# Weights split four blocks deep, and a stage that ends and begins with four blocks by token halves

## The reference, cut to what matters

```
h    = rmsnorm(hres, g0);  m = mixer(h)            # layer 0: attention, layer 1: gated short convolution
hres = hres + rmsnorm(m, g1)                       # a "post norm"
h    = rmsnorm(hres, g2);  m = (relu(h @ w_up))**2 @ w_down
hres = hres + rmsnorm(m, g3)
```

## Time and profile before

| | |
|---|---|
| time, median of 3 runs | 1764.56 us (1763.05 to 1765.94) |
| the profiled execution | 1752.25 us, its span 1750.5 us |
| TensorE matmul busy | 1647.5 us, 94% of the span, mean granted clock 0.978 of full |
| VectorE, ScalarE, GpSimd busy | 771.9, 621.7, 623.2 us |
| raw weights moved | 225 loads of 512 KB |
| share of the chain that ended last | TensorE 79%, VectorE 12%, GpSimd 3%, waiting for nothing shown 3% |

### The profile page before, as it was taken

One profiled execution on the slowest core, in us unless ns is written; L12 is line 12 of the kernel. 1 busy time (PEld: TensorE's weight loads), 2 busy tenths in 40 slices (PEclk: granted clock), 3 DMA queues, 4 the chain that ended last, 5 costly groups with the idle time before them and its releaser, 6 DMA issues.

```text
span 1750.5 us, 31301 instructions
## 1 busy us (share of the span) xinstructions
PE 1647.5 (94%) x12544; PEld 1444.2 (83%) x12544; DVE 771.9 (44%) x1260; ACT 621.7 (36%) x1127; POOL 623.2 (36%) x315
## 2 busy tenths in 40 slices
PE   7999998889999999989998999999998999999895
PEld 6788886879999999989987788888887777777764
DVE  3333333274323141374435642323217897445536
ACT  5455655253223131242223432323224454222222
POOL 2222220354443443454434444444444434700011
PEclk9999997999999999999999999999999999999998
DMA  5111110212323223212222233222331222100001
GB/s 189 56 49 49 49 49 13 73 49 97 90 92 97 86 95 96 76 59 96 85 85 71 73 96 96 94 89 94 97 96 49 85 85 84 50 2 3 2 25 48
DMA packets 35401, 125.66 MB, mean 72 GB/s; under 512 B 3920, under 2 KB 4048, under 8 KB 35280
## 3 DMA queue, kind: packets, MB, share of 16 engines
q1 hardware_dynamic: 35280, 123.90, 22.1%
HBM read 121.79 MB, written 2.10 MB: 71 GB/s over the span
## 4 chain that ended last, share of the span: by engine, by line
PE 79%; DVE 12%; POOL 3%; issue 3%; ACT 2%; DMA 0%; DVEq 0%; SPq 0%; POOLq 0%; ACTq 0%
PE G L1327 63%; PE G L1564 3%; PE PV L1564 3%; PE PV L1441 2%; DVE t L895 2%; PE ST L1564 2%; DVE rstd L830 1%; DVE xl L836 1%; POOL wlo L440 1%; PE PO L1564 1%; PE ST L1300 1%; PE ST L1416 1%; PE G L1414 1%; PE G L1416 1%; PE PO L1430 1%
## 5 line engine op out<-in xcount | busy, mean ns | idle before, releaser
L440 POOL TENSOR_TENSOR wlo<-raw,whi 128x1024 fp32r<-128x1024 f32 x225 | 547.5, 2434 | 1068.1 <-ACT whi L500 663.2
L1327 PE MATMUL G<-xh,whi 128*128 128x256 f32 (+3 forms) x1552 | 385.8, 312 | 4.5 <-POOL wlo L440 2.7
L1327 PE MATMUL G<-xl,whi 128*128 128x256 f32 (+3 forms) x1552 | 368.2, 301 | 0.0
L1327 PE MATMUL G<-xh,wlo 128*128 128x256 f32 (+3 forms) x1552 | 366.5, 300 | 0.0
L1327 PE MATMUL G<-ah,whi 128*128 128x258 f32 (+2 forms) x992 | 270.5, 320 | 10.2 <-POOL wlo L440 5.7
L1327 PEld LDWEIGHTS G<-xh,whi 128*128 128x128 f32 x1552 | 251.2, 189 | 30.5 <-issue 11.8
L511 ACT ACTIVATE whi<-raw 128x1024 fp32r<-128x1024 f32 x112 | 118.8, 1060 | 429.6 <-PE G L1327 429.6
L1327 PE MATMUL G<-al,whi 128*128 128x258 f32 (+2 forms) x992 | 267.7, 317 | 0.0
L1327 PE MATMUL G<-ah,wlo 128*128 128x258 f32 (+2 forms) x992 | 267.6, 317 | 0.0
L1327 PEld LDWEIGHTS G<-xl,whi 128*128 128x128 f32 x1552 | 250.5, 189 | 12.1
L1327 PEld LDWEIGHTS G<-xh,wlo 128*128 128x128 f32 x1552 | 251.6, 189 | 10.2
(11 more groups left out here) (275 smaller groups left out, 2036.0 us busy)
## 6 DMA issues: line engine op xcount, KB each, us to landing
raw<-weights_dram SPq DMA_DIRECT2D x225, 512.0 KB, 3.5
hres<-xT_dram SPq DMA_DIRECT2D x8, 264.0 KB, 6.7
out_dram<-hres SPq DMA_DIRECT2D x8, 256.0 KB, 2.1
con<-consts_dram SPq DMA_DIRECT2D x1, 512.0 KB, 9.5
mat<-mats_dram SPq DMA_DIRECT2D x1, 512.0 KB, 10.3
con<-consts_dram SPq DMA_DIRECT2D x1, 392.0 KB, 6.3
vec<-vecs_dram SPq DMA_DIRECT2D x1, 203.0 KB, 2.4
```

What stands on the lines that cost most here:

```text
L440: nc.gpsimd.tensor_tensor(wlo[:, s % 2], raw[:, s], whi[:, s % 2].bitcast(F32), ALU.subtract)\
L1327: last_of[0] = nc.tensor.matmul(to[:, p0:p1], wt[:, w, ws], xt[:, k, t0 - off:t1_ - off], start=k == 0 and q == 0, stop=k == KT - 1 and q ...
```

## The change

The weights' buffers become `raw` 2, `whi` 4, `wlo` 4 deep: `split(b)` waits for block b-4, and load b for the remainder of b-2. In a transition the old product's blocks 4 to 7 run by token halves, in the four banks of `G` (first all four first halves, then the second halves). The new product's blocks 0 to 3 run by halves in banks of their own: blocks 0 and 1 row by row together, then 2 and 3; where a product has over 512 tokens the second halves lie in PO, PV and the two banks of ST. TensorE's second `post_stat` moves behind row 4 of the first half. VectorE scales `m` in place, adds it to `hres` itself, and makes the remainders of the new product's first four weight blocks (`low_w`); GpSimd does neither in a transition. ScalarE's rows, old squares and splits are interleaved by hand. The tiles of blocks 0 to 3 are read from their banks (`held_tile`), in two pieces where the tokens are over 512. In the wide projection TensorE has blocks 0 to 3 before the first features and 4 and 5 where 2 and 3 were. `x2h` and `x2l` lose the 16 meta columns, and six buffers of the last block share memory with others.

```diff
-        raw = sb("raw", [P, 4, D])
-        whi = sb("whi", [P, 2, D], F32R)
-        wlo = sb("wlo", [P, 2, D], F32R)
+        raw = sb("raw", [P, 2, D])
+        whi = sb("whi", [P, 4, D], F32R)
+        wlo = sb("wlo", [P, 4, D], F32R)
...
             def load(b, j, s):
-                sp.wait_ge(lo_ready, b - 3)
+                sp.wait_ge(lo_ready, b - 1)
...
             done = 0                                      # GpSimd
-            for i, (b, cols) in enumerate(((B_MLP[0], NEED), (B_CI, NEED), (B_MLP[1], OUT), (B_IN2, OUT))):
-                blocks(pool, done, b + 1 - done, low)
-                residual(i, 0, cols)
-                low(b + 1, 1, (b + 1) % 4)
-                residual(i, 1, cols)
-                done = b + 2
+            for b in (B_MLP[0], B_CI, B_MLP[1], B_IN2):
+                blocks(pool, done, b - done, low)
+                done = b + HELD
...
+                for j in range(HELD, KT):                 # ScalarE, post_squares
+                    half_square_of(j, 0)
+                stat_root(s - 1, cols, 0)
+                split(new, 0)
+                half_square_of(4, 1)
+                input_row(0, 0)
+                input_row(1, 0)
+                half_square_of(5, 1)
+                split(new + 1, 1)
+                input_row(2, 0)
+                input_row(3, 0)
+                half_square_of(6, 1)
+                split(new + 2, 2)
+                input_row(4, 0)
+                input_row(5, 0)
+                half_square_of(7, 1)
+                split(new + 3, 3)
+                input_row(6, 0)
+                stat_root(s - 1, cols, 1)
+                input_row(7, 0)
+                stat_root(s, cols, 0)
+                for k in range(KT):
+                    input_row(k, 1)
+                stat_root(s, cols, 1)
...
+                def scaled(k, half):                      # VectorE, last_tiles
+                    nc.vector.scalar_tensor_tensor(m[:, k, o], m[:, k, o], gain(*norm, k), rstd[:, s % 2, tokens(cols, half)],
+                                                   ALU.mult, ALU.mult).then_inc(t1_ready, 1)
+                def residual(k, half):
+                    dve.wait_ge(t1_ready, 2 * KT * i + KT * half + k + 1)
+                    nc.vector.tensor_tensor(hres[:, k, c], hres[:, k, c], m[:, k, tokens(cols, half, cols[0])], ALU.add)\
+                        .then_inc(h_ready, 1)
+                def input_rows(ks, half):
+                    for k in ks:
+                        if k + 1 < KT:
+                            scaled(k + 1, half)
+                        residual(k, half)
+                        if k >= 1:
+                            low_x(i + 1, *pre, k - 1, cols, half)
...
+                stat_recip(s, cols, 0)
+                half_tile(4, 1)
+                dve.wait_ge(rstd_ready, stat_count(s, 0))
+                scaled(0, 0)
+                input_rows((0, 1), 0)
+                half_tile(5, 1)
+                add_square(i, 4, cols, 1)
+                low_w(new)
+                input_rows((2, 3), 0)
+                half_tile(6, 1)
+                add_square(i, 5, cols, 1)
+                low_w(new + 1)
+                input_rows((4, 5), 0)
+                half_tile(7, 1)
+                add_square(i, 6, cols, 1)
+                low_w(new + 2)
+                input_rows((6, 7), 0)
+                stat_recip(s, cols, 1)
+                low_x(i + 1, *pre, KT - 1, cols, 0)
+                low_w(new + 3)
+                stat_recip(s + 1, cols, 0)
+                dve.wait_ge(rstd_ready, stat_count(s, 1))
+                scaled(0, 1)
+                input_rows(range(KT), 1)
+                low_x(i + 1, *pre, KT - 1, cols, 1)
                 stat_recip(s + 1, cols, 1)
...
+                def start(j):                             # TensorE, first_blocks
+                    pe.wait_ge(lo_ready, b0 + j + 1)
+                    pe.wait_ge(tile_out, b0 + j - 3)
                 for half in range(2):
+                    if half == 0:
+                        start(0)
+                        start(1)
+                    for k in range(KT):
+                        pe.wait_ge(x_ready, x_base(i + 1) + KT * half + k + 1)
+                        stat_tile(s, k, cols, half)
+                        for j in range(2):
+                            rows(j, [k], half)
+                        if k == 4 and half == 0:
+                            post_stat(s - 1, cols, 1)
+                    for j in range(2, HELD):
+                        rows(j, range(KT), half)
...
+                for j in range(HELD, KT):                 # TensorE, last_blocks
+                    pe.wait_ge(half_out, HELD * i + j - HELD + 1)
+                    if j == HELD:
+                        rows(j, range(3), 1)
+                        post_stat(2 * i + 1, cols, 0)
+                    rows(j, range(3 if j == HELD else 0, KT), 1)
```

More of the change, by code:

```diff
@@ L437, in low @@
                 pool.wait_ge(hi_ready, b + 1)
-                if not isinstance(b, int) or b >= 2:
-                    pool.wait_ge(block_done, b - 1)
-                nc.gpsimd.tensor_tensor(wlo[:, s % 2], raw[:, s], whi[:, s % 2].bitcast(F32), ALU.subtract)\
+                if not isinstance(b, int) or b >= 4:
+                    pool.wait_ge(block_done, b - 3)
+                nc.gpsimd.tensor_tensor(wlo[:, s], raw[:, s % 2], whi[:, s].bitcast(F32), ALU.subtract)\
                     .then_inc(lo_ready, 1)
-            def residual(i, half, cols):
-                for k in range(KT):
-                    n = 2 * KT * i + KT * half + k + 1
-                    pool.wait_ge(t1_ready, n)
-                    c = tokens(cols, half)
-                    nc.gpsimd.tensor_tensor(hres[:, k, c], hres[:, k, c], t1[:, k % 2, tokens(cols, half, cols[0])], ALU.add)\
-                        .then_inc(h_ready, 1)
-            done = 0
-            for i, (b, cols) in enumerate(((B_MLP[0], NEED), (B_CI, NEED), (B_MLP[1], OUT), (B_IN2, OUT))):
-                blocks(pool, done, b + 1 - done, low)
-                residual(i, 0, cols)
-                low(b + 1, 1, (b + 1) % 4)
-                residual(i, 1, cols)
-                done = b + 2
-            blocks(pool, done, B_O2 + 2 - done, low)
+            done = 0
+            for b in (B_MLP[0], B_CI, B_MLP[1], B_IN2):
+                blocks(pool, done, b - done, low)
+                done = b + HELD
+            blocks(pool, done, B_O2 + 3 - done, low)
             pool.wait_ge(tile_out, B_IN2 + 17)
@@ L567, in mlp @@
-            def mlp(layer, cols, i):
+                    if half:
+                        act.wait_ge(tile_out, b0 + j + 1)
+                    else:
+                        act.wait_ge(half_out, HELD * i + j - HELD + 1)
+                    before = j - 2 if half == 0 or j - 2 >= HELD else None
+                    if before is not None:
+                        act.wait_ge(psq_added, POST_ADD * i + half_added(before, half))
+                    nc.scalar.activation(sq[:, j % 2, c], m[:, j, c], ACT.Square).then_inc(psq_ready, 1)
@@ new lines, in input_row @@
+                def input_row(k, half):
+                    c = tokens(cols, half)
+                    act.wait_ge(h_ready, 2 * KT * i + KT * half + k + 1)
+                    hi = x2h[:, k, tokens(cols, half, META)] if layer == 2 else xh[:, k, c]
+                    nc.scalar.activation(hi, hres[:, k, c], ACT.Copy, scale=gain(layer, n, k)).then_inc(x_hi, 1)
+                    if k >= 2:
+                        act.wait_ge(sq_used, sq_base(s) + KT * half + k - 1)
+                    nc.scalar.activation(sq[:, k % 2, tokens(cols, half, cols[0])], hres[:, k, c], ACT.Square)\
+                        .then_inc(sq_ready, 1)
@@ L835, in low_x @@
                 hi, lo = (x2h, x2l) if layer == 2 else (xh, xl)
-                nc.vector.scalar_tensor_tensor(lo[:, k, c], hres[:, k, c], gain(layer, n, k), hi[:, k, c].bitcast(F32),
+                o = tokens(cols, half, META) if layer == 2 else c
+                nc.vector.scalar_tensor_tensor(lo[:, k, o], hres[:, k, c], gain(layer, n, k), hi[:, k, o].bitcast(F32),
                                                ALU.mult, ALU.subtract).then_inc(x_ready, 1)
@@ L863, in out_tiles, with low_w @@
                 blocks(dve, b0, 8, body)
+            def low_w(b):
+                dve.wait_ge(hi_ready, b + 1)
+                nc.vector.tensor_tensor(wlo[:, b % 4], raw[:, b % 2], whi[:, b % 4].bitcast(F32), ALU.subtract)\
+                    .then_inc(lo_ready, 1)
             def last_tiles(i, b0, cols, before, norm, pre):
                 s = 2 * i + 1
+                new = b0 + KT
                 def half_tile(j, half):
-                    _, _, p0, p1 = part(cols, half)[0]
                     if half:
@@ L1391, in product @@
                     done = 4 + (n - 4) // 4 * 4
-                for j in range(done, n if end is None else n - 2):
+                for j in range(done, n if end is None else n - HELD):
```

250 lines of the change are left out of this document (111 added, 139 removed).

## The result

The changed kernel takes 1749.03 us at the median (1748.12 to 1753.46, 4 runs) beside 1763.92 for the kernel before: a ratio of 0.9928, interval 0.9903 to 0.9952. Measured again beside the experiments it was 1743.89 against 1762.38, 0.9889 (0.9845 to 0.9932). It is faster by 15 to 19 us, where 31 were forecast; the time lies inside the range. The profiled executions differ less, 1746.8 us of span against 1750.5, for a reason shown under the experiments (the clock of the last stretch).

The account below looks back on a forecast made before the run. TensorE's matmuls fill 94% of the span; the holes are transitions, chained through VectorE. Transitions 29.5 plus projection 2.4 less start 0.5 make 31.4 us: 1764.6 - 31.4 = 1733 us, range 1717 to 1751.

Parts of the forecast that it names:

- the transitions: Four transitions, TensorE waiting in a chain through VectorE: some 12 us lost in each, 29.5 us forecast back together.
- scaled rows: VectorE's rows in transitions: 0.47 us duration throughout once GpSimd is idle, against 0.86 beside a GpSimd add.
- the add: VectorE's add onto hres in transitions: 0.35 us from start to start, 0.82 if as slow as on GpSimd.
- The start: Kernel start, third block's split and remainder come among the first rows: 0 to 2.4 us lost, 0.5 taken.
- The projection's 2.4 us: Attention's output projection: the 2.42 us wait for its third block's remainder goes with four-deep buffers, 2.4 us gained.
- the 9.9 of the sum: Attention's output projection and transition 0: forecast gains of 2.4 us and 7.5 us.
- the 12.3 us between profiled execution and runs: Whole kernel: the runs shown lay 12.3 us above the profiled execution's 1752.25 us, and the forecast carried this over.
- the step that failed: Attention, ScalarE's block wait gone and GpSimd's remainders moved: between 2.4 us lost and 2.4 gained, 0 taken.
- VectorE as the bound: Rival, transitions: scaled rows stay 0.79 us or low_w and add are slower; 17 us gained, 1747 us; 15%.
- the second rival: Behind the transitions the third tile isn't late, so block 4's 2.6 us waits go: up to 10 us more, 1723 us; 10%.
- the third: Rival, long runs of blocks: loads come late with raw two deep, kernel slower, 1769 us or more; 5%.
- The gain taken back behind the transitions: Rival, behind the transitions: VectorE stays a tile behind, gain lost tile by tile; 0 to 3 us gained; 4%.

Follow-up runs that it names:

- all three edits: Changed kernel with attention's ScalarE wait put back, the fifth block waiting for the second tile, VectorE making 15 wide-projection remainders: 1713.44 us, 0.9728.
- second profile of before: Kernel before, rerun with no edit for its granted clocks and another profile: 12 runs, 1749.96 to 1767.95 us; profile at clock 0.970, rest 326.3 us.

## Why the prediction was wrong

**Right: the transitions.** Forecast gains of 7.5, 7.6, 8.0 and 6.4 us from old block 4 on; measured 7.1, 8.0, 8.0 and 6.8. The steps held too: scaled rows 0.48 us throughout, the add 0.42 (I took it as the sum of squares), low_w 1.22 (1.13), three waits of 0.6 us or less at the first-half rows and one of 2.7 to 2.8 before the fifth block in transitions 0 and 2 (2.6). The start cost 0.6 (0.5). The projection's 2.4 us is not shown by itself: its column's 11.2 us come near the 9.9 of the sum in part by luck, since the first profile of before ran there at the lower clock for longer. Carrying over the 12.3 us between profiled execution and runs was right: that profile had the last stretch at a clock of 0.96, most of the kernel's timed runs have a lower mean clock, and the profiles of the changed kernel itself have 0.87 and 0.88.

**Wrong, the step that failed:** "In attention ScalarE no longer waits for block s, and GpSimd's remainders move: between 2.4 lost and 2.4 gained, I take 0." It costs 13.9 us (10 to 14 over all profiles). I priced one remainder once; it is met seven times, of which six cost: 1.75 us in each of three heads (34.55 us against 32.8), 3.3 in two (36.1), 1.7 behind the last. The further 1.5 in the two is the lower clock, seen in attention only in kernels whose coefficient or difference is held. The bound of one remainder's length was right for one meeting and wrong by the number of heads. Nor did I ask which VectorE instruction stood within 0.7 us of the remainder's new start, though the trace's order of both engines would have answered it. The Trainium skill, "SBUF — State Buffer", section "SBUF: two separate sides", has the reason: whichever of a VectorE operation with two SBUF inputs and a GpSimd operation starts first gets the pair of ports for its whole instruction. The trace agrees down to one element per partition: 2.05 us for a coefficient of 0.22, started 0.33 us behind the remainder. To within some 0.1 us the starts on record don't tell which was first: with the remainders written out GpSimd's start is 0.04 us behind that of the difference, and the difference was held. I used that rule for the transitions, where the change takes GpSimd away, and for al behind them, and not where the change moves GpSimd.

**Missing: the wide projection.** The sum ended at the first scan. Behind it VectorE is the bound (busy 60.3 of 61.2 us before), and the change lets GpSimd run up to four remainders ahead, so they come in bunches: 5.1 us given back, 3.3 of it in held instructions and 1.8 in a wait for TensorE's tile. With VectorE making the remainders no instruction was held and the 5.1 came back, at a clock of 1.00; with all three edits, at 0.95 as in the changed kernel, 3.8 did. Whether the 1.8 us is the lower clock's alone stays open.

**The rivals.** VectorE as the bound (1747 us) came nearest in time and is still wrong in its reason: no scaled row stayed at 0.8. That the time lies inside the range is luck in the same sense: the range reaches so far because of that rival. The third tile was late (2.8 and 2.7 us), against the second rival, and loads were not, against the third. The gain taken back behind the transitions came true for the last one only, where the wide projection gave back 5.1 of 6.8 us. Not foreseen: the rest, at like clock, is some 2 to 3 us shorter, of which I know only that it isn't the transitions.

The terms nearly close. Set against the second profile of before, whose rest ran at like clock, the columns add up to 0.3 + 14.4 - 29.2 + 5.1 - 3.6 = -13.0 us (start, attention, the four columns, wide, rest); the two measured differences are 14.9 and 18.5.

## What to carry to other kernels

An edit that lets an engine run earlier also moves what runs behind it. Where GpSimd and VectorE work out of the same memory, write down for every repeated stage which VectorE instruction of the chain stands within a microsecond of GpSimd's new start, and multiply one meeting by the number of repetitions before calling it nothing. When a stretch's length is compared between two profiles, compare its clock first: here one column of the same kernel differed by 4.4 us between two profiles. To mend such a place, make the engine that has time wait for the instruction it would hold, or give the work to the engine that would be held.

## What the runs showed of the hardware

A shift of 0.17 us in GpSimd's start decided between 0.37 and 2.54 us for the same VectorE instruction. VectorE's instructions that read a tile of PSUM and one of SBUF were not held: in the wide projection of the changed kernel a remainder runs from 1351.25 to 1353.72, the read-out of a tile (z<-G,rstd) starts at 1351.38 and takes 0.68 us, as it does elsewhere, and the difference of two tiles of SBUF behind it, at 1351.98, takes 2.30 in place of 0.68. And runs of the kernel before, made beside one another, spread over 1.3%, with mean granted clocks of 0.968 to 0.982 (between TensorE's two levels of 1.2 and 2.4 GHz, near the upper): 1747.55 us at 0.982, 1770.95 at 0.969.
